# Mixer one of a two-block model on one core: small columns, log decays and gate rows computed inside the channel-major projection stage, third modulation part inside the context norm

## The reference, cut to what matters

```python
mod_x = (silu(c) @ ada_w + ada_b)            # six parts of 1024: shift, scale, gate, shift, scale, gate
mod_c = (silu(c_ctx) @ ada_w + ada_b)
zx = modulate(rmsnorm(x, norm1_g), sh1x, sc1x) @ w_in      # 1024 latent tokens
zc = modulate(rmsnorm(ctx, norm1_g), sh1c, sc1c) @ w_in    # 256 context tokens
gq, gk, gv, gg, glr, mqk, mv, mo, mi, mf = split(z)        # glr: 32 columns, mi and mf: 8 each
log_a = log_sigmoid(glr @ gla_up_w + gla_up_b) / 16        # GLA log decays, per direction
ig, lf = mi + ml_i_b, log_sigmoid(mf + ml_f_b)             # mLSTM gates: prefix sums and running maxima follow
```

## Time and profile before

| | |
|---|---|
| time, median of 3 runs | 3931.68 us (3930.94 to 3936.35) |
| the profiled execution, its own time | 3930.38 us |
| its span in the trace | 3928.6 us |
| mean granted TensorE clock, share of full | 0.908 |
| PE busy / DVE busy / ACT busy | 3262.0 / 2150.1 / 1266.6 us |

### The profile page before, as it was taken

One profiled execution on the slowest core, in us unless ns is written; L12 is line 12 of the kernel. 1 busy time (PEld: TensorE's weight loads), 2 busy tenths in 40 slices (PEclk: granted clock), 3 DMA queues, 4 the chain that ended last, 5 costly groups with the idle time before them and its releaser, 6 DMA issues. The chain is left out here.

```text
span 3928.6 us, 50808 instructions
## 1 busy us (share of the span) xinstructions
PE 3262.0 (83%) x18300; PEld 2611.3 (66%) x18300; DVE 2150.1 (55%) x3022; ACT 1266.6 (32%) x1898; POOL 210.6 (5%) x301
## 2 busy tenths in 40 slices
PE   5799963876789999995799788768579989998977
PEld 2687743764468888883687687547358877887755
DVE  3211824445389999995311284475437765776443
ACT  3202203342368888884100142422121100110111
POOL 1000000340011111110000000000000000000000
PEclk8899975898889999997899899879789999999989
DMA  6233631581377769982232211100203322332121
GB/s 242 71 91 96 199 129 36 161 239 61 123 268 295 281 261 375 367 316 91 86 96 76 101 38 49 57 2 3 88 28 93 91 80 91 91 91 86 64 64 43
DMA packets 377629, 502.81 MB, mean 128 GB/s; under 512 B 47513, under 2 KB 284432, under 8 KB 374176
## 3 DMA queue, kind: packets, MB, share of 16 engines
q1 hardware_dynamic: 341488, 439.53, 33.1%
q10 hardware_dynamic: 23520, 42.21, 3.1%
q0 software_dynamic: 12496, 19.35, 1.4%
HBM read 449.14 MB, written 74.92 MB: 133 GB/s over the span
## 5 line engine op out<-in xcount | busy, mean ns | idle before, releaser
L1936 DVE TENSOR_TENSOR exp_w_lo<-exp_w_raw,exp_w_hi 128x1024 fp32r<-128x1024 f32 x378 | 435.5, 1218 | 4.9
L1884 ACT ACTIVATE exp_w_hi<-exp_w_raw 128x1024 fp32r<-128x1024 f32 x378 | 370.9, 1055 | 7.7 <-PE exp_up_psum L339 7.7
L337 PE MATMUL in_ps_psum<-hN_hi,in_wh 128*128 128x512 f32 x704 | 275.4, 391 | 38.4 <-DVE in_wl L331 38.4
L337 PE MATMUL up_ps_psum<-hN_hi,up_wh 128*128 128x512 f32 x704 | 281.1, 399 | 30.8 <-DVE up_wl L331 30.8
L338 PE MATMUL up_ps_psum<-hN_lo,up_wh 128*128 128x512 f32 x704 | 280.7, 399 | 0.0
L339 PE MATMUL up_ps_psum<-hN_hi,up_wl 128*128 128x512 f32 x704 | 280.6, 399 | 0.0
L338 PE MATMUL in_ps_psum<-hN_lo,in_wh 128*128 128x512 f32 x704 | 274.9, 390 | 0.0
L339 PE MATMUL in_ps_psum<-hN_hi,in_wl 128*128 128x512 f32 x704 | 274.8, 390 | 0.0
L329 DVE CAST in_wh<-in_w 128x1024 fp32r<-128x1024 f32 x44 | 30.6, 694 | 387.9 <-PE in_ps_psum L339 378.0
L337 PE MATMUL exp_up_psum<-exp_w_hi,exp_x_hi 128*128 128x512 f32 x592 | 231.6, 391 | 3.9 <-DVE exp_w_lo L1936 3.9
L339 PE MATMUL exp_up_psum<-exp_w_hi,exp_x_lo 128*128 128x512 f32 x592 | 231.1, 390 | 0.0
(11 more groups left out here) (628 smaller groups left out, 7345.9 us busy)
## 6 DMA issues: line engine op xcount, KB each, us to landing
exp_w_raw<-in_expert_w_in SPq DMA_DIRECT2D x256, 512.0 KB, 5.7
up_w<-in_ffn_up SPq DMA_DIRECT2D x88, 512.0 KB
exp_w_raw<-in_expert_w_out SPq DMA_DIRECT2D x64, 512.0 KB, 6.8
hF<-in_expert_w_out SPq DMA_DIRECT2D x64, 512.0 KB
ada_w<-in_ada_w SPq DMA_DIRECT2D x24, 1024.0 KB, 5.6
in_w<-in_w_in SPq DMA_DIRECT2D x44, 512.0 KB
down_w<-in_ffn_down SPq DMA_DIRECT2D x44, 512.0 KB
wout_w<-in_w_out SPq DMA_DIRECT2D x16, 512.0 KB
```

The lines of the kernel that those rows point to most:

```text
L337: pe.matmul(out, r(w[0]), r(x[0]), start=start, stop=False)
L1884: act.activation(wh[:, c, :].bitcast(F32R), raw[c], ACT.Copy).then_inc(s_wh, 1)
L1936: dve.tensor_tensor(wl[:, c, :].bitcast(F32R), raw[c], wh[:, c, :], ALU.subtract).then_inc(s_wl[c], 1)
```

## The change

`stage_misc` and `stage_gates` are gone. `stage_gemm_f` is replaced for "in1" by a new `stage_project`, which runs the small columns as a first product, then the same 20 tiles, with the log decays of chunk t after tile t (t < 10), the gate work in steps after tiles 2 to 12, and the chunk sums of the log decays after tile 13. The gate rows stand on 40 partitions of 128 tokens per direction in place of 4 partitions of 1280, with a short chained scan over the chunk ends. The log decays are stored to DRAM by POOL and loaded per unit by `stage_gla`. Modulation part 2 moves beside "n1c"; the rings of parts 1 and 2 and of `stage_values` have 3 tiles in place of 4.

```diff
-    A, name, NR, NW, R = K.A, f"ada{g}", 4, 512, 2 if g == 0 else 1
+    A, name, NR, NW, R = K.A, f"ada{g}", (4, 3, 3)[g], 512, 2 if g == 0 else 1
...
+def stage_project(K, tiles):
...
+            @block.gpsimd
+            def _(pool):
...
+                pool.wait_ge(s_sev, 2)
+                for n in range(2):
+                    r = [small[64 + 32 * n + 4 * d:64 + 32 * n + 4 * d + 4, :] for d in range(2)]
+                    pool.dma_start(gate_dram[n, 0], r[0]).then_inc(s_gst, 16)
+                    pool.dma_start(gate_dram[n, 1][:, 0:T], r[1][:, NCTX:TALL]).then_inc(s_gst, 16)
+                    pool.dma_start(gate_dram[n, 1][:, T:TALL], r[1][:, 0:NCTX]).then_inc(s_gst, 16)
+                pool.wait_ge(s_gst, 96)
+                for n, t in enumerate((gi, gf)):
+                    for d in range(2):
+                        pool.dma_start(t[half[d], :], gate_dram[n, d].rearrange("h (c t) -> (h c) t", t=P)).then_inc(s_gin, 16)
+                def decays(ns):
+                    for n in ns:
+                        pool.wait_ge(s_lf, n + 1)
+                        pool.dma_start(la_dram[n * P:(n + 1) * P, :], la[:, n, :]).then_inc(s_lst, 16)
...
+            @block.tensor
+            def _(pe):
...
+                def logits(n):
+                    if n == 0:
+                        pe.wait_ge(s_sev, 2)
+                        pe.wait_ge(s_up, 96)
+                    else:
+                        pe.wait_ge(s_lb, n)
+                    pe.matmul(pl[:], small[0:LOGIT_ROWS, n * P:(n + 1) * P], upw[:], start=True, stop=True).then_inc(s_lg, 1)
...
+                def sums():
+                    pe.wait_ge(s_lf, NCH)
+                    pe.wait_ge(s_cc, 6)
+                    for k in range(2 * NCH):
...
+                            mm = pe.matmul(pg[:, o:o + 2], la[:, c, (2 * d + p) * P:(2 * d + p + 1) * P], K.c(f"ends{d}"), start=True, stop=True)
+                    mm.then_inc(s_sum, 1)
+                pe.wait_ge(s_swl, 1)
+                product(0, 1).then_inc(s_smm, 1)
+                for t in range(NT):
+                    u = t % 2
+                    pe.wait_ge(s_wl[u], t // 2 + 1)
+                    if t >= 2:
+                        pe.wait_ge(s_ev[u], t // 2)
+                    elif u == 0:
+                        pe.wait_ge(s_sev, 2)
+                    product(u, tiles[t][4]).then_inc(s_mm[u], 1)
+                    if t < NCH:
+                        logits(t)
+                    if t == 4:
+                        chunk_ends()
+                    if t == 7:
+                        previous()
+                    if t == 10:
+                        columns()
+                    if t == 13:
+                        sums()
...
+            @block.vector
+            def _(dve):
...
+                for t in range(NT):
+                    if t + 2 < NT:
+                        weights(t + 2)
+                    if t < NCH:
+                        biased(t)
+                    if 1 <= t <= NCH:
+                        log_decay(t - 1)
+                    if t == 3:
+                        scans()
+                    if t == 5:
+                        chained()
+                    if t == 8:
+                        maxima()
+                    if t == 12:
+                        columns()
+                    if t == 14:
+                        summed()
...
+            @block.scalar
+            def _(act):
...
+                for t in range(NT):
...
+                    evict(t)
+                    if t < NCH:
+                        log1p(t)
+                    if t == 2:
+                        gate_log1p()
+                    if t == 9:
+                        gate_exp()
...
-    R, W, NB, NR, NC, NK = 16, 64, 4, 4, D // P, 4
+    R, W, NB, NR, NC, NK = 16, 64, 4, 3, D // P, 4
...
-        loads = lambda k: 64 if isx(k) else 32
+        loads = lambda k: 80 if isx(k) else 48
...
-        la = lambda k: K.la[:, scan(k) % NCH, units[k][1] * 256:(units[k][1] + 1) * 256]
+        la = lambda k: lb[k % NB]
...
+                    c, d = scan(k) % NCH, units[k][1]
+                    sp.dma_start(lb[b][:], log_decay[c * P:(c + 1) * P, d * 256:(d + 1) * 256]).then_inc(s_in[b], 16)
...
                 def decay(k):
                     d, u = units[k][1], k % 2
+                    pe.wait_ge(s_in[k % NB], arrived(k))
                     if k >= 2:
                         pe.wait_ge(s_exp, k - 1)
...
-                for k, (_, d) in enumerate(units):
-                    for p in range(2):
-                        mm = pe.matmul(pends[:, k, p, :], la(k)[:, p * P:(p + 1) * P], K.c(f"ends{d}"), start=True, stop=True)
-                mm.then_inc(s_pend, 1)
...
-            stage_norm(K, "n1c", K.ctxF, K.ctx, NCTX, g1, shift=mc[:, 48:56], scale=mc[:, 56:64])
+            stage_norm(K, "n1c", K.ctxF, K.ctx, NCTX, g1, shift=mc[:, 48:56], scale=mc[:, 56:64], ada=2)
...
-        stage_misc(K)
...
-    stage_gates(K)
     stage_gla(K)
```

More of the change, by code:

```diff
@@ L650, in _ @@
+                pool.wait_ge(s_ex, 3)
+                for n, t in enumerate((urow, wrow)):
+                    for d in range(2):
+                        pool.dma_start(rows_dram[d, n].rearrange("h (c t) -> (h c) t", t=P), t[half[d], :]).then_inc(s_rows, 16)
+                decays(range(8, NCH))
+                pool.wait_ge(s_rows, 64)
+                pool.wait_ge(s_lst, 16 * NCH)
             @block.sync
             def _(sp):
[L652 to L653 removed]
@@ L664, in _, with product @@
[L664 to L670, removed]
+                def product(u, with_ctx):
+                    for h in range(NH + with_ctx):
+                        x = K.x if h < NH else K.ctx
+                        n, c = (BANK, slice(h * BANK, (h + 1) * BANK)) if h < NH else (NCTX, slice(0, NCTX))
+                        for k in range(KT):
+                            mm = matmul3(pe, pm[u][:, h, 0:n], (wh[u][:, k, :], wl[u][:, k, :]), (x[0][:, k, c], x[1][:, k, c]),
+                                         start=k == 0, stop=k == KT - 1)
+                    return mm
@@ new lines, in maxima @@
+                def maxima():
+                    dve.wait_ge(s_mcol, 1)
+                    step = Count(dve, s_gv, 0, 13)
+                    step(dve.tensor_copy(mcol[:], pg[0:R, 0:1]))
+                    step(dve.scalar_tensor_tensor(mrun[:], acum[:], mcol[:], mloc[:], ALU.add, ALU.max))
+                    step(dve.tensor_tensor(urow[:], acum[:], mrun[:], ALU.subtract))
+                    step(dve.tensor_tensor(crow[:], gi[:], acum[:], ALU.subtract))
+                    for d in range(2):
+                        step(dve.tensor_copy(uend[half[d], :], urow[half[d], end[d]:end[d] + 1]))
+                    assert step.n == 19
@@ new lines, in _ @@
+                dve.wait_ge(s_sw, 64)
+                split(dve, wt[0][:], wh[0][:], wl[0][:], s_swh, 1).then_inc(s_swl, 1)
+                weights(1)
+                for t in (acum, mloc, uend, ends, mcol, mprev, cr):
+                    dve.memset(t[:], 0.0).then_inc(s_gv0, 1)
+                dve.memset(ca[:], -1e30).then_inc(s_gv0, 1)
+                dve.memset(cm[:], 0.0).then_inc(s_gv0, 1)
+                dve.wait_ge(s_gv0, 9)
+                weights(0)
+                for t in range(NT):
[15 more added lines that the diff above has]
+                        summed()
@@ new lines, in log1p, with gate_log1p @@
+                def log1p(n):
+                    act.wait_ge(s_lb, n + 1)
+                    if n >= 2:
+                        act.wait_ge(s_lf, n - 1)
+                    step = Count(act, s_la, 0, 3 * n)
+                    l = le[n % 2]
+                    step(act.activation(l[:], la[:, n, :], ACT.Abs))
+                    step(act.activation(l[:], l[:], ACT.Exp, scale=-1.0))
+                    step.mark(act.activation(l[:], l[:], ACT.Ln, bias=1.0))
+                def gate_log1p():
+                    act.wait_ge(s_gin, 64)
+                    step = Count(act, s_ga)
+                    step(act.activation(gt[:], gf[:], ACT.Abs))
+                    step(act.activation(gt[:], gt[:], ACT.Exp, scale=-1.0))
+                    step.mark(act.activation(gt[:], gt[:], ACT.Ln, bias=1.0))
@@ new lines, in _ @@
+                act.wait_ge(s_smm, 1)
+                flat = pm[0][:].rearrange("p a b -> p (a b)")
+                act.activation(small[:, NCTX:TALL], flat[:, 0:T], ACT.Identity, bias=sbias[:]).then_inc(s_sev, 1)
+                act.activation(small[:, 0:NCTX], flat[:, T:TALL], ACT.Identity, bias=sbias[:]).then_inc(s_sev, 1)
+                for t in range(NT):
+                    if t and tiles[t][2] != tiles[t - 1][2]:
+                        act.preload_act_table_set("silu_and_others" if tiles[t][2] == ACT.Silu else "sigmoid_and_others")
+                    evict(t)
[5 more added lines that the diff above has]
+                        gate_exp()
```

326 lines of the change are left out of this document (162 added, 164 removed).

## The result

| | before | after |
|---|---|---|
| time, median | 3931.31 us (3929.3 to 3936.35, 4 runs) | 3862.73 us (3861.62 to 3871.59, 4 runs) |
| span of the profiled execution | 3928.6 us | 3860.6 us |

The ratio is 0.9825, 95% interval 0.9812 to 0.9838: 68.6 us faster. The forecast was 3843 with a range up to 3859. The direction was right, the gain was 20 us smaller than forecast, and the time lies 4 us outside the range. Both kernels ran in one group; the experiments ran later in three groups with a run of the kernel before in each (medians 3936.66, 3934.64 and 3934.56 us).

The account below looks back on a forecast made before the run. PE was taken to bound the projection. The terms -144.6 + 16.7 + 1 + 42.5 + 4.5 - 12 + 3.5 summed to -88.4 us, giving 3842.0 for a profiled execution and a median of 3843, range 3831 to 3859.

Parts of the forecast that it names:

- What bounds the kernel: Whole kernel: PE sets the end of the projection; DVE, ACT and POOL work there is free while PE never waits.
- part 2 in the context norm: Modulation part 2 run beside the context norm: that stage ends at 148.1 in place of 131.38, +16.7 us.
- GLA's start: GLA stage up to its first decay product: without the sums it waits only for three loads, saving 13.6 us.
- GLA, steady: GLA's repeated units: the wait for loads at each decay lengthens them, +3.5 us in all, bounds 0 and 9.
- Late by 0.5: GLA units: loads ready at 4.8 us, wanted at 4.34; each unit grows by half the lateness, 14 x 0.25.
- the head: GLA from first decay product to first output: first latent units need their loads earlier, +1.5 us.
- Logits: Projection: ten logit chunks between dense products at full clock, 0.86 us each, +8.6 us, bounds 8.6 to 17.
- Chunk sums: Projection after tile 13: 80 records, clock falling halfway, and a slow start of tile 14; 14 us, bounds 8.6 and 18.7.
- Tile 0: Projection's first tile: slow first matmuls move into the small columns' product, -1.5 us; PE waits for tile 0's weights, +2.0.
- Rings of three: Weight rings of 3 tiles in place of 4: values stage +4.5 us, bounds 2 and 7; modulation part 1 +1.
- Rival 4: Projection: gate chain over DRAM is late for ACT if POOL's issues are slow; 3850 us at 5 us each, chance 0.04.
- Rival 5: Projection no longer bound by PE, the logits' chain through DVE and ACT sets it; 3932 us and more, chance 0.02.

## Why the prediction was right in sign and short in size

- **What bounds the kernel**, the removed 144.6 us, part 2 in the context norm (+17.2 for +16.7) and GLA's start (-13.2 for -13.6) held.
- **GLA, steady, is the step that failed.** The prediction put it as "their traffic ends at about 716.25, 4.1 us after PE's point", from one unit whose traffic ended clean. A median set of five ends 5.1 us after its first issue, some at 6.6, and the kernel before already had a set of over 5 us, hidden by its slack. "Late by 0.5" became up to 1.92, and "half of it" for each unit, 0.25, became 0.6 of pure waiting: PE waited at 8 of 13 decay products, 8.0 us together. Behind the longest wait the granted clock was 0.72 (625 to 631 us) and that unit took 6.0 us, some 1.6 more than one without a wait, a term the sum did not have. Together +11.3 for +3.5, and +5.6 for +1.5 in the head. The mechanism was the right one: with the load landing first and waited for alone, 67.5 us came back to the tenth. I had named "a GLA unit is over 5 us" as what would prove me wrong; it was 5.3, (682.1 - 618.4) / 12 between first and last steady decay products.
- **Logits**, 8.6 forecast: the work is 8.6, stepping out and back is 4.3 more, a term the sum did not have.
- **Chunk sums**, 14 forecast: 13.6 and 1.9 behind them. The clock did fall, as the earlier trace rows suggested, and they need not have been dear: in parts they cost 9.1 (8.5, and 6 x 0.11 in the tiles behind).
- **Tile 0**: "The slow first matmuls lie in it now and not in tile 0" failed in part. In this profile they lie in both, since the clock fell again behind the 2.15 us pause (2.0 forecast): small product, pause and tile 0 took 31.7 us, where the forecast's terms give 16.1 + 2.0 + 10.9 = 29.0. In the six profiles without that fall they took 28.6 to 29.2, so whether this term held was chance.
- **Rings of three**: +4.5 forecast for the values and 6.6 measured, +1 for part 1 and 2.7 measured; four tiles give 5.0 and 1.3 of these back.
- **Rival 4**, the gate chain: POOL's ten gate issues took 0.51 to 0.54 us each, its last gate load was issued at about 186 us, and ACT took up `gate_log1p` at 222.6. It never came near. DVE was idle during all of these issues but the first, so they are no test of issues beside a busy DVE; three later ones with DVE at work (at 236.6, 266.8 and 309.2 us) took 0.54 us, as those without. **Rival 5**: PE was busy for 265.65 of the 265.70 us of tiles 0 to 19 and what stands between them.

## What to carry to other kernels

When an edit moves a wait for a group of loads earlier, take the landing from the slowest of many groups, since slack in the old kernel hides the tails; and give what is needed first its own semaphore and the first place in the queue, or issue it earlier (here 13 to 17.5 us for a few lines). Small PE work is cheapest in short pieces between dense products, as long as the pieces are few: each stepping out and back for a logit costs 0.4 us, while a single long run of it, here 80 records, lets the clock fall. A pause of 2 us ahead of dense work can cost twice its length (3.6 to 4.5 us here, in four profiles of ten).

## What the runs showed of the hardware that was not expected

- The time from issue to landing of loads of 128 KB in one queue grew with their place in the set: 2.1, 2.2, 2.8 and 3.3 us. In some sets the last load landed 4.3 to 4.8 us after its issue, 1.5 us later than in the others; in the kernel before, the traffic was down to 5 to 10 GB/s while such a last piece came in.
- PE at the 2.4 GHz level, after a pause of 2.15 us, ran on at that level for less than 1 us and only then fell to the 1.2 GHz level, in four of ten profiles. In GLA it fell behind a wait of 1.92 us.
- Eighty records of full weight loads with two columns each, PE busy throughout, took the mean clock to 0.66, with 0.11 us from one record to the next up to the 33rd and 0.21 behind it; in parts of 12 to 16 records between dense products it stayed at 1.00.
